# Moving a quarter product of a block-triangular inverse into an earlier visit to tile mode

## What is computed

```python
decay = jnp.exp(jnp.where(causal, g[..., :, None] - g[..., None, :], -jnp.inf))
lower = jnp.einsum('bhnid,bhnjd->bhnij', k_beta, k) * decay * strict
a_mat = lower + jnp.eye(C, dtype=f32)
sol = lax.linalg.triangular_solve(a_mat, rhs, left_side=True, lower=True, unit_diagonal=True)
u, w = sol[..., :Dv], sol[..., Dv:]
...
def step(S, inp):
    v_new = u_c - jnp.einsum('bhck,bhkv->bhcv', w_c, S)
    ...
    S = S * jnp.exp(gl_c)[..., None, None] + jnp.einsum('bhck,bhcv->bhkv', kt_c, v_new)
```

## Time and profile before

| what | value |
|---|---|
| median of three runs | 1895.36 us |
| the profiled execution | 1896.67 us |
| its span | 1894.9 us |
| PE busy | 1849.9 us (98%), 12873 matmuls |
| DVE busy | 1548.5 us (82%) |
| ACT busy | 862.5 us (46%) |
| start to start of two heads in the middle (L1316 to L1316) | 50.5 us |

### The profile page before, as it was taken

One profiled execution on the slowest core, in us unless ns is written; L12 is line 12 of the kernel. 1 busy time (PEld: TensorE's weight loads), 2 busy tenths in 40 slices (PEclk: granted clock), 3 DMA queues, 4 the chain that ended last, 5 costly groups with the idle time before them and its releaser, 6 DMA issues.

```text
span 1894.9 us, 34073 instructions
## 1 busy us (share of the span) xinstructions
PE 1849.9 (98%) x12873; PEld 1674.8 (88%) x12873; DVE 1548.5 (82%) x3086; ACT 862.5 (46%) x1515; POOL 780.1 (41%) x574
## 2 busy tenths in 40 slices
PE   6999999999999999999999999999999999999998
PEld 3779999999877999999999898888888888888886
DVE  4577777777665889988795789989889899998998
ACT  3525445454332324588887333333343333333333
POOL 0000000000043434887784354555555565555652
PEclk9999999999999999999999999999999999999999
DMA  9732222222451425777677999999999999999984
GB/s 394 278 110 81 85 77 81 84 74 85 160 196 70 145 67 181 226 222 226 196 223 219 345 372 390 388 383 391 379 373 386 390 384 372 374 380 374 370 337 152
DMA packets 179730, 474.74 MB, mean 251 GB/s; under 512 B 16752, under 2 KB 79184, under 8 KB 176240
## 3 DMA queue, kind: packets, MB, share of 16 engines
q1 hardware_dynamic: 133488, 304.78, 45.7%
q0 software_dynamic: 46080, 167.79, 23.1%
HBM read 426.57 MB, written 45.94 MB: 249 GB/s over the span
## 4 chain that ended last, share of the span: by engine, by line
PE 55%; DVE 10%; issue 1%; DMA 1%; POOL 1%; ACT 0%; DVEq 0%; ACTq 0%
PE dd L2832 18%; PE pp L2819 16%; PE pp L2832 9%; PE pp L2439 7%; PE dd L2787 4%; DMA x<-in_v,idx 1%; POOL hot_a L2599 1%; DVE top_i L2482 1%; DVE top_i L2471 1%; DVE top L3077 1%; DVE less L2472 1%; DVE top_v L2466 1%; DVE top_v L2477 1%; PE pp L468 1%; DVE cand L3189 1%
## 5 line engine op out<-in xcount | busy, mean ns | idle before, releaser
L452 ACT ACTIVATE w_hi<-w_raw 128x1024 fp32r<-128x1024 f32 x202 | 212.9, 1054 | 156.2 <-PE pp L468 99.5
L468 PE MATMUL pp<-act_hi,w_hi 128*128 128x272 f32 x1040 | 234.0, 306 | 2.9 <-ACT qt L2885 1.2
L456 DVE TENSOR_TENSOR w_lo<-w_raw,w_hi 128x1024 fp32r<-128x1024 f32 x173 | 212.8, 1231 | 27.7 <-ACT w_hi L452 27.6
L468 PE MATMUL pp<-act_hi,w_lo 128*128 128x272 f32 x1040 | 215.1, 288 | 0.0
L468 PE MATMUL pp<-act_lo,w_hi 128*128 128x272 f32 x1040 | 214.7, 288 | 0.0
L3014 ACT ACTIVATE co_hi<-cf 128x384 fp32r<-128x384 f32 x126 | 66.3, 527 | 320.1 <-PE pp L2832 257.6
L2819 PE MATMUL pp<-act_hi,w_hi 128*128 128x384 f32 x616 | 208.8, 339 | 0.0
L2819 PE MATMUL pp<-act_lo,w_hi 128*128 128x384 f32 x616 | 207.6, 337 | 0.0
L2599 POOL TENSOR_SCALAR hot_a<-cst,gcols 128x128 f32<-128x128 f32 x144 | 191.3, 1336 | 39.4 <-PE dd L2787 39.1
L2819 PE MATMUL pp<-act_hi,w_lo 128*128 128x384 f32 x616 | 207.1, 336 | 0.0
L468 PEld LDWEIGHTS pp<-act_hi,w_hi 128*128 128x128 f32 x1040 | 161.9, 189 | 17.5 <-issue 10.4
(11 more groups left out here) (498 smaller groups left out, 4595.2 us busy)
## 6 DMA issues: line engine op xcount, KB each, us to landing
w_raw<-in_stream SPq DMA_DIRECT2D x206, 512.0 KB
v_raw<-in_v SPq DMA_DIRECT2D x128, 512.0 KB
ada_w<-in_ada SPq DMA_DIRECT2D x24, 1024.0 KB, 10.7
gt<-gate_matrix SPq DMA_DIRECT2D x31, 768.0 KB
gate_matrix<-gstage SPq DMA_DIRECT2D x11, 2048.0 KB, 10.3
early<-cst SPq DMA_DIRECT2D x50, 192.0 KB, 4.0
cst<-early SPq DMA_DIRECT2D x50, 192.0 KB
wrow<-in_wout SPq DMA_DIRECT2D x8, 512.0 KB, 8.2
```

The costliest lines, as they stand in the source:

```text
L452: nc.scalar.activation(w_hi[k.slot][:], w_raw[k.slot][:], ACT.Copy).then_inc(w_hi_done, 1)
L456: nc.vector.tensor_tensor(w_lo[k.slot][:], w_raw[k.slot][:], w_hi[k.slot][:].bitcast(F32), ALU.subtract).then_inc(w_lo_done, 1)
L468: last = nc.tensor.matmul(pp[s][:, b, 0:HN], w[:, c * P:(c + 1) * P], a[:, c, b * HN:(b + 1) * HN], start=(c == 0 and w is w_hi[s] and a i ...
```

## The change

The first quarter product of the last level no longer has a visit of its own. It is split by associativity over the 32-blocks: in the join visit, `lt`'s blocks 2 and 3 against columns 0 and 1 are multiplied by the inverses of the blocks 0 and 1 (four products of 32x32 for each chunk, L1324 of the changed kernel), and block 1's inverse by the upper pair (L1319, one product for each chunk that moves 64 columns). ACT copies three regions of PSUM to one tile `joins` (`first_join`, `cross`, `last_join`; L1546 to L1548). The joined visit gets two products of 32x32 for each chunk (L1336) in place of the one that made the turned joined block. DVE subtracts their result from `cross` (L1819), and the second quarter product of 64x64 (L1345) follows. `ti_lo`, its two copies on DVE (L1814), its negation (L1818) and ACT's copy to `a5` are gone. The table `PIECES` is changed with it.

```diff
-        PIECES = {... "level 3": 3, "level 4": 1, "joined 4": 3, "level 5": 2, "joined 5": 1, ...
+        PIECES = {... "level 3": 3, "level 4": 2, "joined 4": 2, "joined 5": 3, ...
...
-                    pe.wait_ge(ti_ready, 3 * hv + 2)
-                    for c in range(NC):
-                        for b in (1, 3):
-                            t = c * P + B4 * b
-                            last = nc.tensor.matmul(dd[strip(b), 1, strip(c)], lt[strip(b - 1), t:t + B4],
-                                                    tic[strip(b - 1), strip(c)], start=True, stop=True,
-                                                    tile_position=(B4 * (b - 1), B4 * b))
-                    last.then_inc(a4_done, 1)
-                    beside("level 4")
-                    pe.wait_ge(a4_ready, hv + 1)
+                    pe.wait_ge(ti_ready, 2 * hv + 2)
                     gate_pe(pe, qkm_ready, hv + 1)
                     for c in range(NC):
+                        t, hi = strip(c), c * P + B2
+                        for b, bank in ((1, 1), (3, 3)):
+                            nc.tensor.matmul(dd[strip(b), bank, t], lt[strip(b - 1), c * P + B4 * b:c * P + B4 * (b + 1)],
+                                             tic[strip(b - 1), t], start=True, stop=True, tile_position=(B4 * (b - 1), B4 * b))
+                        nc.tensor.matmul(dd[strip(1), 2, c * B2:(c + 1) * B2], tic[strip(1), t], lt[strip(1), hi:hi + B2],
+                                         start=True, stop=True, tile_position=(B4, B4))
+                        for b in (2, 3):
+                            for g in range(2):
+                                to = slice(c * B2 + B4, (c + 1) * B2) if g else t
+                                last = nc.tensor.matmul(dd[strip(b), 1 + g, to], lt[strip(g), c * P + B4 * b:c * P + B4 * (b + 1)],
+                                                        tic[strip(g), t], start=True, stop=True, tile_position=(B4 * g, B4 * b))
+                    last.then_inc(joins_done, 1)
+                    beside("level 4")
+                    pe.wait_ge(joins_ready, 3 * hv + 3)
+                    for c in range(NC):
                         t = strip(c)
-                        nc.tensor.matmul(dd[strip(1), 2, t], ty[strip(1), 0, t], a4[strip(1), t], start=True, stop=True,
-                                         tile_position=(B4, B4))
-                        for b in (3, 1):
-                            last = nc.tensor.matmul(dd[strip(b - 1), 3, t], a4[strip(b), t], ty[strip(b), 0, t], start=True,
-                                                    stop=True, tile_position=(B4 * b, B4 * (b - 1)))
+                        for b, a in ((3, last_join), (1, first_join)):
+                            nc.tensor.matmul(dd[strip(b - 1), 3, t], a[strip(b), t], ty[strip(b), 0, t], start=True,
+                                             stop=True, tile_position=(B4 * b, B4 * (b - 1)))
+                        for b in (2, 3):
+                            at = c * B2 + B4 * (b - 2)
+                            last = nc.tensor.matmul(dd[strip(b), 2, t], cross[strip(1), at:at + B4], first_join[strip(1), t],
+                                                    start=True, stop=True, tile_position=(B4, B4 * b))
                     last.then_inc(t21_done, 1)
                     beside("joined 4")
 
-                    pe.wait_ge(ti_ready, 3 * hv + 3)
-                    for c in range(NC):
-                        t = slice(c * B2, (c + 1) * B2)
-                        last = nc.tensor.matmul(dd[HI, 1, t], lt[LO, c * P + B2:(c + 1) * P], ti_lo[LO, t],
-                                                start=True, stop=True)
-                    last.then_inc(a5_done, 1)
-                    beside("level 5")
                     pe.wait_ge(tu_ready, 2 * hv + 1)
                     gate_pe(pe, a5_ready, hv + 1)
...
-                    act.wait_ge(a4_done, hv + 1)
-                    nc.scalar.activation(a4[:], dd[:, 1, 0:TC], ACT.Copy).then_inc(a4_ready, 1)
+                    act.wait_ge(joins_done, hv + 1)
+                    nc.scalar.activation(cross, dd[:, 2, 0:2 * TC], ACT.Copy).then_inc(joins_ready, 1)
+                    nc.scalar.activation(first_join, dd[:, 1, 0:TC], ACT.Copy).then_inc(joins_ready, 1)
+                    nc.scalar.activation(last_join[strip(3), :], dd[strip(3), 3, 0:TC], ACT.Copy).then_inc(joins_ready, 1)
                     beside("level 4")
-                    act.wait_ge(a5_done, hv + 1)
-                    nc.scalar.activation(a5[HI, :], dd[HI, 1, 0:2 * TC], ACT.Copy).then_inc(a5_ready, 1)
...
-                    dve.wait_ge(ti_ready, 3 * hv + 2)
-                    for b in range(2):
-                        nc.vector.tensor_copy(by_chunk(ti_lo[strip(b), :])[:, :, strip(b)], by_chunk(tic[strip(b), :]))
                     inside(3)
                     beside("level 3")
                     dve.wait_ge(t21_done, hv + 1)
-                    nc.vector.tensor_scalar(by_chunk(ti_lo[strip(1), :])[:, :, strip(0)], by_chunk(dd[strip(1), 2, 0:TC]), -1.0, None,
-                                            ALU.mult).then_inc(ti_ready, 1)
                     st.settle()
                     for b in (0, 2):
                         last = nc.vector.tensor_scalar(in_chunks(tu[strip(b), :], b + 1), by_chunk(dd[strip(b), 3, 0:TC]), -1.0, None,
                                                        ALU.mult)
                     last.then_inc(tu_ready, 1)
+                    nc.vector.tensor_tensor(by_chunk(cross[HI, :])[:, :, strip(0)], by_chunk(first_join[HI, :]),
+                                            by_chunk(dd[HI, 2, 0:TC]), ALU.subtract).then_inc(a5_ready, 1)
```

More of the change, by code:

```diff
@@ L271, in build @@
                 yl, tic = sb("yl", [P, TP // 4], stack=st2), sb("tic", [P, TP // 4], stack=st2)
-                apc, a4 = sb("apc", [P, TP // 4], stack=st2), sb("a4", [P, TP // 4], stack=st2)
-                ti_lo, a5 = sb("ti_lo", [P, TP // 2], stack=st2), sb("a5", [P, TP // 2], stack=st2)
+                apc = sb("apc", [P, TP // 4], stack=st2)
+                joins = sb("joins", [P, TP], stack=st2)
                 folded_c = sb("folded_c", [P, 7, P // 4], stack=st2)
-                sb("levels_apart", [P, 7 * TP - 7 * TP // 4 - TP - 7 * P // 4], stack=st2)
+                sb("levels_apart", [P, 7 * TP - 10 * TP // 4 - 7 * P // 4], stack=st2)
                 k_tail = sb("k_tail", [P, TP], stack=st2)
@@ L1037, in build @@
             sem("dty_done"))
-        a4_done, a4_ready, t21_done, a5_done, a5_ready, t5_done, folded_ready, ti_zero = (
-            sem("a4_done"), sem("a4_ready"), sem("t21_done"), sem("a5_done"), sem("a5_ready"), sem("t5_done"),
-            sem("folded_ready"), sem("ti_zero"))
+        joins_done, joins_ready, t21_done, a5_ready, t5_done, folded_ready = (
+            sem("joins_done"), sem("joins_ready"), sem("t21_done"), sem("a5_ready"), sem("t5_done"), sem("folded_ready"))
         ks_done, r_ready, vn_done, vn_ready, o_done, ds_done, s_ready = (
@@ L1093, in correct @@
             return last
+        first_join, cross, last_join = joins[:, 0:TC], joins[:, TC:3 * TC], joins[:, 3 * TC:4 * TC]
         def by_two(t):
@@ L1122, in build @@
         PIECES = {"start": 4, "beta": 1, "turned": 2, "inverse": 2, "products": 3, "level 0": 4, "level 1": 3, "level 2": 3,
-                  "level 3": 3, "level 4": 1, "joined 4": 3, "level 5": 2, "joined 5": 1, "scan 0": 1, "state 0": 1,
+                  "level 3": 3, "level 4": 2, "joined 4": 2, "joined 5": 3, "scan 0": 1, "state 0": 1,
                   **{f"residual {c}": 2 for c in range(1, NC)}, **{f"scan {c}": 1 for c in range(1, NC)},
@@ L1163, in _ @@
                 retire(pool, ended)
-                nc.gpsimd.memset(ti_lo[:], 0.0).then_inc(ti_zero, 1)
                 def keep(k, col):
@@ L1283, in head @@
                     beside("inverse")
-                    pe.wait_ge(ti_ready, 3 * hv + 1)
+                    pe.wait_ge(ti_ready, 2 * hv + 1)
                     if has_prior(hv):
@@ L1343, in head @@
                         t = slice(c * B2, (c + 1) * B2)
-                        last = nc.tensor.matmul(dd[LO, 3, t], a5[HI, t], tu[HI, c * P + B2:(c + 1) * P],
+                        last = nc.tensor.matmul(dd[LO, 3, t], cross[HI, t], tu[HI, c * P + B2:(c + 1) * P],
                                                 start=True, stop=True)
@@ L1809, in head @@
                                                ALU.mult))
-                    if not has_prior(hv):
-                        dve.wait_ge(ti_zero, 1)
-                    dve.wait_ge(ti_ready, 3 * hv + 2)
-                    for b in range(2):
-                        nc.vector.tensor_copy(by_chunk(ti_lo[strip(b), :])[:, :, strip(b)], by_chunk(tic[strip(b), :]))
                     inside(3)
```

## The result

Seven runs of the changed kernel gave 1898.24 to 1902.31 us, median 1900.52; seven of the kernel before 1893.65 to 1898.01, median 1896.91. The ratio is 1.0020 with a 95% interval of 1.0011 to 1.0029: slower, by 0.2%. So the sign is settled and the size is 4 to 6 us, where +1.2 had been forecast. One of e2's eleven runs took 2277 us, at a granted clock of 0.75; no ratio counts it.

What follows compares the result with a forecast made beforehand. PE's queue bounds the heads, with DVE's list close behind. Head 0 -0.54, head 1 +0.36, five heads +0.25 each, head 7 +0.1 sum to +1.2 us on the median 1895.36: 1896.5 us, range 1893.0 to 1901.5.

Steps and rivals of the forecast that it cites:

- within 0.2%: Whole kernel: time changes by no more than about 3.8 us, what a measurement can tell from no change; chance 0.79.
- the likeliest case: Whole kernel: the forecast with its lower end, 1894.8 to 1897 us, 1893 to 1899 with single-run scatter; chance 0.77.
- the hindered case: Join and joined visits: tiles hinder each other in part or wholly, up to 1903.6 us; chance 0.15.
- The visits: PE in each head: one visit goes, join visit 0.23 us longer, joined visit 0.02 longer; PE alone 0.54 us shorter.
- The visit that goes: PE in each of 8 heads: the dropped visit, with entering and leaving, costs 0.79 us.
- The slower rival: Join and joined visits: tiles of one strip don't overlap, 0.88 us more a head, 1903.6 us; chance 0.15 including partial hindering.
- The moved wait: DVE in head 2: joined visit starts one piece later, so DVE waits 0.42 us and its list down to L1829 shifts.
- The 0.05 us that I took off the list: DVE from L1818 to L1648: three instructions remain, perhaps with one semaphore gap less, so 0.05 us shorter.
- the 0.25 us of heads 2 to 6: Heads 2 to 6: each 0.25 us longer, as PE stands still 0.8 us before L1362 though it has less to do.
- Head 1: Head 1: no slack between DVE and PE at L1362, so 0.36 us longer, PE's wait there 1.1 us.
- Head 7: Head 7: the low part of an output chunk comes about 0.95 us later; net cost 0.1 us or so.
- Everything behind the heads is not touched.: Stages after the heads: no change; a later-stage shift from the program's different length, of either sign, had chance 0.03.

Runs made afterwards that it cites:

- e2: Changed kernel with two DVE steps (last gating product of the previous head, one convolution tap) moved behind the end of the inverse: 1894.26 us, 0.9991 of the kernel before.
- e5: Kernel before with 20 more matmuls in each head, written into parts of PSUM that nobody reads: 1897.82 us, ratio 1.0010.
- e1: Changed kernel timed again without an edit, beside the kernel before: 1901.16 us, ratio 1.0032.
- e6: Changed kernel with a POOL memset of the same size kept at the start of the head stage: 1900.33 us, ratio 1.0023 to the kernel before.
- e4: Changed kernel with pieces 1, 3, 3 in place of 2, 2, 3 at the three places: 1897.42 us, ratio 1.0010 to the kernel before.
- e9: e2 timed again to pool its times: 1894.21 us, ratio 0.9993 to the kernel before.
- e8: e2 with head 7's gating product also moved behind the end of the inverse: 1892.91 us, ratio 0.9989 to the kernel before.
- e3: Kernel before with the same two DVE steps moved as in e2: 1895.59 us, ratio 1.0000.

## Why the prediction was right, and where it was too small

The measured time lies in the range of 1893.0 to 1901.5, and the mechanism is the one forecast: the place, PE's wait at L1363 in six heads, 0.74 us in head 2 (0.8 forecast), DVE's wait for the joined visit in every head, head 0 alone shorter. But +1.2 us was a third of what came, or less, and "within 0.2%" with 0.79 was too sure. That 1900.52 us lies in the range is in part luck: the likeliest case alone was given as 1893 to 1899, and only half of the hindered case, which did not come, stretched it to 1901.5. Step by step:

- *The visits.* Head 0, where PE alone decides, is 0.52 shorter (0.54 forecast). The join visit: 0.65 for 0.60, so 0.28 more than before and not 0.23. The joined: 0.38 for 0.39. The visit that goes was thus worth 0.52 + 0.28 + 0.01 = 0.81 for 0.79. Seven tiles, of which three read strip 1 and three write strip 3, overlap. The slower rival, tiles that hinder each other, is wrong. The Trainium skill's rule in "TensorE: Matmul & The Clock Gate", section "The mechanism", that a weight load overlaps running matmuls only in another row group, was given a small share; by it the joined visit, with three tiles on one row group, would have grown by 0.44 us, and it grew by 0.01 over the three-tile visit's 0.37.
- *The moved wait.* DVE delayed by 0.42; measured 0.49 (the visit's 0.05 more, and 0.02 in the handover). The 0.05 us that I took off the list isn't there (4.95 for 4.94).
- *The restart.* This term was missing. In the kernel before, the weights of L1362 start to load at 252.31, beside running matmuls and 0.11 us ahead of their own at 252.42. After PE has stood still, load and matmul of L1363 both stand at 251.08: nothing is hidden. L1363 takes 0.49 us for 0.38, and from it to the next L1363, 4.23 us pass (251.08 to 255.31 below) for 4.11 (252.42 to 256.53). That is 0.11 us in each of five heads. In head 1 it was there before too: L1362 took 0.49.

```profile
255.31 0.38 PE L1363 MATMUL dd<-r_new,tu 128*128 128x128 f32 x2
```

- Together 0.07 + 0.06 + 0.11 make the 0.25 us of heads 2 to 6 into 0.49 (measured 0.49 to 0.57), and 5 x 0.25 into 2.5. Head 1 was forecast +0.36 and is +0.18: the 0.35 us for which DVE stood before L1829 aren't there before L1825, and PE's wait in it is 0.74, not 1.1. Head 7: +0.21 in its last part for 0.1. The heads: **+2.4 for +1.2**.
- *"Everything behind the heads is not touched."* This sentence is the one that failed; only a chance of 0.03 had been left for it. The wait for `v_lo` at 1050 us and what goes with it cost 0.75 us in the changed trace (the matmuls of the last stage are 0.50 us earlier than before ahead of it, and 0.25 later behind), and the time outside the span grows by 0.65. e5 shows that both come when 20 matmuls a head are added to the old program.

2.4 + 0.75 + 0.65 = 3.8 us, which stands beside 3.6 (first comparison), 5.8 (e1) and 4.6 (e6). For the others the same sum, with their own heads, gives:

| | the sum | measured |
|---|---|---|
| e4 | -0.3 | +2.1 |
| e5 | +3.6 | +2.1 |
| e2, e9 | -2.4 | -1.1, -1.1 |
| e8 | -2.9 | -2.4 |

Most leftovers lie within an interval's 1.7 to 2.2 us, and they have both signs. Those of e1 (+2.0) and e4 (+2.4) lie just outside, and for these two the granted clock gives most of the reason, by an estimate. Averaged over their runs it was 0.9940 and 0.9938, and 0.9950 for the kernel before beside them. One short fall of the clock, as in the last section, takes (1 - 0.61) x 4 = 1.6 us at full clock off a span of 1895, 0.0008, and costs 1.1 to 1.3 us. So e1 had one fall more in a run and e4 between one and two, worth about 1.5 and 1.8 us. Why these two sets had more of them isn't shown, and how the other leftovers are shared out stays open: -1.5 us for e5, +1.3 for e2 and e9. Open too is by what way a longer program moves a load at 1050 us. The traces show that ACT waited longer for `v_raw` there, 4.4 to 4.5 us in the kernel before and e3, 5.7 to 6.1 in all nine of the longer program. Before and after:

```profile
1049.75 1.06 ACT L3002 ACTIVATE v_hi<-v_raw 128x1024 fp32r<-128x1024 f32 x1 [4.47 <-DMA v_raw<-in_v]
```
```profile
1050.57 1.06 ACT L2998 ACTIVATE v_hi<-v_raw 128x1024 fp32r<-128x1024 f32 x1 [5.75 <-DMA v_raw<-in_v]
```

and that the instruction queue moves a little more (105 packets for 103):

```profile
q8 instruction: 105, 1.72, 0.4%
```

That one causes the other was not tried.

## What to carry to other kernels

When an engine is 100% busy but another follows it at a distance of 0.1 us, shortening the first pays 0.1 us and no more: look for the engine that has no wait in the window, and measure the distance at the place where the two meet. Before work is moved in front of a handover, list everything that is queued behind that handover on the other engine; here one piece of 0.76 us moved ahead of it cost 0.6 us in each of six heads (e1 against e4), and two small steps moved out of DVE's list turned +2.4 us into -3.8. Here a wait cost its length and a restart of 0.11 us, and with 20 more matmuls a head came 0.75 us in a stage that they don't touch and 0.65 outside the span.

## What the runs showed of the hardware

- **The granted clock falls for a short stretch after PE has stood still, in some executions and not in others.** PE waits 2.7 us at L1269 (at about 119 us) in every kernel, and right behind it the clock fell in five of the eleven traces (before, e1, e4, e5, e6). Busy time from 120 to 124 us in the kernel before, and in the changed one (the last columns are clock, DMA share and GB/s):

```profile
120.00:124.00 4.00, 4.00 (x24) 4.00 (x23) 2.29 (x5) 2.21 (x5) 0.33 (x2) 0.61 0.02 5
```
```profile
120.00:124.00 4.00, 4.00 (x36) 4.00 (x35) 2.31 (x6) 2.21 (x5) 0.34 (x2) 1.00 0.02 4
```

  In the same 4 us, 24 matmuls for 36. The mean of 0.61 is a mixture of the two levels, 1.2 and 2.4 GHz. L1309 in head 0 starts at 142.8 us in the one and at 141.4 in the other, and L1269 at 119.6 and 119.4: so the stretch costs 1.1 us. The kernel before had a second, which costs 1.3 us and which the changed one doesn't have:

```profile
576.00:580.00 4.00, 4.00 (x24) 4.00 (x24) 3.79 (x7) 1.35 (x3) 0.00 (x0) 0.64 0.02 4
```

  The two together are 2.4 us, as much as the heads differ by. This is why the two profiled spans are only 0.2 us apart: a comparison of single spans would have called the change free.
- **Tiles don't keep step.** In the join visit the 32-column tiles run on to the next chunks while the tile with 64 columns is behind: by 242.97 us, 12 of the 16 passes of L1317 have begun, those of three chunks, and 3 of the 8 of L1319. The visit costs 0.65 us for 28 products, hardly more than 16 products on four tiles with 64 columns, 0.58.
